# Expert weights of a mixture-of-experts stage loaded as contraction halves, 16 KB a partition, with stationary operands read at a step of four

## The reference, cut to what matters

```python
def expert_block(args):
    xb, e = args
    g = xb @ w_gate[e].astype(jnp.float32) + b_gate[e].astype(jnp.float32)
    u = xb @ w_up[e].astype(jnp.float32) + b_up[e].astype(jnp.float32)
    g = jnp.minimum(g, SWIGLU_LIMIT)
    u = jnp.clip(u, -SWIGLU_LIMIT, SWIGLU_LIMIT)
    act = g * jax.nn.sigmoid(SWIGLU_ALPHA * g) * (u + 1.0)
    return act @ w_down[e].astype(jnp.float32) + b_down[e].astype(jnp.float32)
```

## Time and profile before

| | us |
|---|---|
| timed executions | 2716.2, 2707.0, 2698.15 |
| their median | 2707.0 |
| profiled execution, span from first to last instruction | 2703.2 |
| TensorE busy in it | 2299.3 |

### The profile page before, as it was taken

One profiled execution on the slowest core, in us unless ns is written; L12 is line 12 of the kernel. 1 busy time (PEld: TensorE's weight loads), 2 busy tenths in 40 slices (PEclk: granted clock), 3 DMA queues, 4 the chain that ended last, 5 costly groups with the idle time before them and its releaser, 6 DMA issues.

```text
span 2703.2 us, 25686 instructions
## 1 busy us (share of the span) xinstructions
PE 2299.3 (85%) x10610; PEld 1330.2 (49%) x10611; DVE 651.8 (24%) x995; ACT 360.4 (13%) x547; POOL 108.4 (4%) x117
## 2 busy tenths in 40 slices
PE   3987789799879999997899979779997957867998
PEld 1643346334333344332344337458846747846873
DVE  2657623111111111110111111510004464621000
ACT  1121011111011111110111121210001321211000
POOL 2000010000000000000000010020000011300000
PEclk9898889999989999998999989889997978878999
DMA  9761245899579999995899994034343400003430
GB/s 230 260 249 48 75 168 193 330 360 394 207 272 396 395 394 394 394 379 188 328 394 394 394 330 148 32 110 156 140 145 119 151 5 1 1 32 110 156 109 16
DMA packets 246162, 580.79 MB, mean 215 GB/s; under 512 B 7123, under 2 KB 8163, under 8 KB 245952
## 3 DMA queue, kind: packets, MB, share of 16 engines
q1 hardware_dynamic: 240272, 562.39, 56.4%
q0 software_dynamic: 5808, 17.19, 2.8%
HBM read 578.48 MB, written 1.07 MB: 214 GB/s over the span
## 4 chain that ended last, share of the span: by engine, by line
PE 76%; DVE 9%; DMA 6%; ACT 5%; issue 3%; SPq 1%; another core or an unknown queue 0%; POOL 0%; DVEq 0%; ACTq 0%
PE ps L1157 17%; PE ps L1448 11%; PE ps L1174 8%; PE ps L1459 6%; PE ps L582 6%; PE ps L590 5%; PE ps L1138 4%; DMA ring<-in_w_up 4%; PE ps L1159 2%; PE ps L1180 2%; PE ps L506 2%; DMA ring<-in_ada_w 2%; PE ps L1793 1%; PE ps L1799 1%; PE ps L803 1%
## 5 line engine op out<-in xcount | busy, mean ns | idle before, releaser
L1157 PE MATMUL ps<-ring,arena 128*64 128x512 f32 x1632 | 367.0, 603 | 37.7 <-issue 32.4
L1448 PE MATMUL ps<-arena,ring 128*128 128x256 f32 x1408 | 308.4, 383 | 1.5 <-ACT arena L559 1.5
L1448 PEld LDWEIGHTS ps<-arena,ring 128*128 128x128 f32 x1408 | 270.2, 192 | 39.7 <-ACT arena L559 2.3
L1157 PEld LDWEIGHTS ps<-ring,arena 128*64 128x64 f32 x1632 | 114.2, 139 | 285.5 <-issue 274.3
L1174 PE MATMUL ps<-ring,arena 128*64 128x512 f32 x1088 | 244.4, 601 | 6.0 <-ACT arena L1127 1.5
L1102 DVE TENSOR_SCALAR arena<-ps 128x512 f32<-128x512 f32 x34 | 23.5, 692 | 619.1 <-PE ps L1159 619.1
L1174 PEld LDWEIGHTS ps<-ring,arena 128*64 128x64 f32 x1088 | 90.4, 138 | 138.3 <-issue 138.3
L1459 PE MATMUL ps<-ring,arena 128*128 128x512 f32 x352 | 151.4, 592 | 0.0
L582 PE MATMUL ps<-arena,ring 128*128 128x256 f32 x672 | 149.2, 384 | 0.7 <-ACT arena L559 0.7
L1138 PEld LDWEIGHTS ps<-arena 128*128 128x128 f32 x1120 | 129.3, 194 | 28.2 <-issue 28.2
L1157 PE MATMUL ps<-arena 128*64 128x512 f32 x544 | 126.7, 620 | 17.3 <-issue 17.3
(11 more groups left out here) (442 smaller groups left out, 2097.3 us busy)
## 6 DMA issues: line engine op xcount, KB each, us to landing
ring<-in_w_up SPq DMA_DIRECT2D x64, 2048.0 KB, 15.0
ring<-in_w_down SPq DMA_DIRECT2D x64, 2048.0 KB, 13.5
ring<-in_w_gate SPq DMA_DIRECT2D x32, 2048.0 KB, 22.4
arena<-in_w_gate SPq DMA_DIRECT2D x32, 2048.0 KB, 22.1
ring<-in_ffn_w_gate_up SPq DMA_DIRECT2D x22, 2048.0 KB, 7.9
ring<-in_ada_w SPq DMA_DIRECT2D x12, 2048.0 KB, 19.9
ring<-in_ffn_w_down SPq DMA_DIRECT2D x10, 2048.0 KB, 7.7
ring<-in_w_in SPq DMA_DIRECT2D x8, 2048.0 KB, 19.8
```

The costliest lines, as they stand in the source:

```text
L1157: pe.matmul(bank(i)[h * CAP:(h + 1) * CAP, :], xT[:, k, 0:CAP], w[h][:, k, :], start=(k == 0), stop=False)
L1448: m = pe.matmul(bank(b0 + g)[:, c * SEQ:(c + 1) * SEQ], w[:, k, (2 * g + c) * P:(2 * g + c + 1) * P], hT2[:, k, :], start=(k == 0), stop=( ...
```

## The change

All six transfers of an expert become halves of the contraction: half h of a matrix is rows 512h to 512h+511, all 1024 columns. In a half, partition p takes rows 4p to 4p+3, which lie side by side in memory, so that a partition gets one run of 16 KB. The number of transfers, their 2 MB, their slots, their order and the waits stay.

Step k of the contraction now is rows 512(k//4) + 4p + k%4 in partition p. So `pe_gate_up` takes block k%4 of half k//4 and the columns of h from it. The gather takes every fourth feature of a half of `h2` as the stationary operand, and the transposes in `pe_hidden` every fourth column of `act_`; a new function `every4` gives these views, with a step of 16 bytes. `pe_down` is unchanged, since its transposed hidden columns come in the new order. The order of the instructions is the same on every engine.

```diff
--- before.py
+++ after.py
@@ -1075,13 +1075,17 @@
 
 
         W7 = [RING[:, i * SLOT_W:(i + 1) * SLOT_W] for i in E_SLOT]
-        gate_w = [[x.rearrange("p (k n) -> p k n", k=KD) for x in xs] for xs in (W7[0:2], odd_gate)]
-        up_w = [W7[2 + h].rearrange("p (k n) -> p k n", k=KD) for h in range(2)]
+        gate_w = [[x.rearrange("p (k n) -> p k n", k=4) for x in xs] for xs in (W7[0:2], odd_gate)]
+        up_w = [W7[2 + h].rearrange("p (k n) -> p k n", k=4) for h in range(2)]
         down_w = [W7[4 + h].rearrange("p (k n) -> p k n", k=4) for h in range(2)]
 
         def slot_iota(r, n):
             a = names["slots"][0] + r * 2 * CAP
             return CON[:, a:a + n]
+
+        def every4(x, j):
+
+            return x.rearrange("p (q j) -> p j q", j=4)[:, j, :]
 
         def dve_choose(dve, s, e, r, odd):
 
@@ -1135,7 +1139,7 @@
             pe.wait_ge(s.p_ready, n)
             for k in range(KD):
                 for t in range(TT):
-                    m = pe.matmul(bank(2 + k // 4)[:, (k % 4) * P:(k % 4 + 1) * P], h2[:, t, k * P:(k + 1) * P], Psel[:, t, :],
+                    m = pe.matmul(bank(2 + k // 4)[:, (k % 4) * P:(k % 4 + 1) * P], every4(h2[:, t, k // 4 * 512:(k // 4 + 1) * 512], k % 4), Psel[:, t, :],
                                   start=(t == 0), stop=(t == 1))
                 if k % 4 == 3:
                     m.then_inc(s.x_ps, 1)
@@ -1154,7 +1158,7 @@
                 weights(i)
                 for k in range(KD):
                     for h in range(2):
-                        pe.matmul(bank(i)[h * CAP:(h + 1) * CAP, :], xT[:, k, 0:CAP], w[h][:, k, :], start=(k == 0), stop=False)
+                        pe.matmul(bank(i)[h * CAP:(h + 1) * CAP, :], xT[:, k, 0:CAP], w[k // 4][:, k % 4, h * 512:(h + 1) * 512], start=(k == 0), stop=False)
                 for h in range(2):
                     m = pe.matmul(bank(i)[h * CAP:(h + 1) * CAP, :], Ee[odd], b_[:, h * 512:(h + 1) * 512], start=False, stop=True)
                 m.then_inc(done, 1)
@@ -1162,7 +1166,7 @@
         def pe_hidden(pe, s, n):
             pe.wait_ge(s.a_ready, n)
             for j in range(4):
-                m = pe.transpose(bank(2)[:, j * P:(j + 1) * P], act_[:, j * P:(j + 1) * P], ident)
+                m = pe.transpose(bank(2)[:, j * P:(j + 1) * P], every4(act_, j), ident)
             m.then_inc(s.aT_ps, 1)
 
         def pe_down(pe, s, n, weights, pwT):
@@ -1280,12 +1284,10 @@
             i = ("w_gate", "w_up", "w_down").index(name)
             w = A[name][0][e:e + 1] if isinstance(e, int) else A[name][0][bass.ds(e, 1)]
             for h in range(2):
-                if i < 2:
-                    src, dst = w[:, :, h * 512:(h + 1) * 512], (gate_w[odd], up_w)[i][h]
-                else:
-                    src, dst = w[:, h * 512:(h + 1) * 512, :], down_w[h]
+                dst = (gate_w[odd], up_w, down_w)[i][h]
                 there = odd_ready[h] if i == 0 and odd else slot_ready[E_SLOT[2 * i + h]]
-                sp.dma_start(dst, src.rearrange("a (k p) n -> p (a k) n", p=P)).then_inc(there, 16)
+                src = w[:, h * 512:(h + 1) * 512, :].rearrange("a (p k) n -> p (a k n)", p=P)
+                sp.dma_start(dst.rearrange("p k n -> p (k n)"), src).then_inc(there, 16)
 
         def sp_s7(sp):
             for i, name in enumerate(("w_gate", "w_up", "w_down")):
```

## The result

The changed kernel takes 2831.75 us (median of four, 2828.66 to 2835.14), the kernel before 2703.01 (of four). The ratio is 1.0467 with a 95% interval of 1.0437 to 1.0496: slower by 129 us. The forecast of 2702 us was wrong, and rival A (2825.5) came true. In the rows of the changed kernel TensorE's lines of the expert stage stand four lower: the gather's L1138 is L1142, and L1157 is L1161.

A forecast was written before the change was run, and what follows sets the result against it. TensorE and the weight transfers were both nearly full, with transfers falling 1.1 us an expert behind. Span 2703.2 - 5.5 (transfer waits) + 0 (strided loads) = 2697.7, plus 3.8 outside the span, gave 2702 us; range 2690 to 2838.

The forecast's parts named there:

- rival A: Strided loads of the stationary operand run at half speed: gathers cost 123 us more, transposes about 1; 2825.5 us; chance 0.37.
- Step (4): Stationary operands of gathers and transposes read at a step of four: zero cost, not firmly; at most 123 and 15 us.
- The last line of the prediction: Signs of being wrong: a gather longer than 3.8 us, or pieces called issue ahead of L1161 over 60 us.
- The bound "a column takes twice as long": Upper bound for strided stationary loads: +110 ns on 1120 gather loads, 123 us, and at most 15 us for transposes.
- Step (1): Weight transfers in 16 KB runs: 610 ns a run, 430 GB/s, an expert in 29.3 us; gain 5.5 us.
- the five waits: TensorE's waits for the w_up transfer late in the expert stage, 5.2 us in all, expected to vanish.
- Step (2): SyncE issues 128 descriptors instead of 1024 or 512 and is free sooner; worth nothing.
- Step (3): Moving side of gate and up matmuls: same count, shape, order and contiguous columns, only addresses differ; zero.
- Rival B: Code fetches ahead of expert matmuls get slower behind 16 KB packets, by 70 us; 2771 us; chance 0.08.
- Step (5): Psel, the outputs in PSUM, the copies and the biases stay as before; zero.
- Rival C: Code fetches get quicker with fewer descriptors in the rings; half of 49.7 us goes; 2673 us; chance 0.05.
- Rival D: Long runs strike memory less evenly, all transfer rates stay at 387 GB/s; 2720 us; chance 0.04.

The follow-up runs named there:

- The first experiment: The changed kernel with its 16 KB runs kept but gather and transposes reading side by side, against the kernel before: 2695.14 us against 2707.61, ratio 0.9964.

## Why the prediction was wrong

Step (4) failed: "It has that much in reserve, and I take zero, but not firmly." The term for the loads of the gathers was put at zero and measured 134.7 us: a load takes 329 instead of 192 ns, 137 more, and 122 of them stand in the pace of the gather. The reasoning took a reserve of one kind for another. That a transpose's load of 128 columns is faster (144 ns in the mean, 141 in the median of the earlier trace rows, against 192) says something of how often or how fast the engine takes a column whose data lie side by side; it says nothing of what a column costs that shares its line with no other. The changed kernel shows both loads growing together, 141 to 213 ns and 192 to 329. The rest of the step's working was sound and gave the case that came true: no cover for a slower load, all 35 gathers on the path, and an upper bound of 110 ns a load where the pace grew by 122. The last line of the prediction named the sign, a gather longer than 3.8 us; it is 7.57. The bound "a column takes twice as long" was too low by a little; it is 1.93/0.86, 2.2 times. The transposes at 1.2 us were seen rightly in rival A.

The Trainium skill's rule in Advanced Engine Details and Errata, section SBUF Cachelines, that at least two hits on a 16-byte line are needed, is borne out by these runs: two hits (a step of two) cost 0.89 ns a column against 0.86, one hit 1.93. The prediction had read it and let an analogy from rows about something else outweigh it. That was the error of judgement.

Step (1), the transfers, held: 611 ns a packet where 610 was worked out, 432 GB/s where 430 was, the five waits gone. The extrapolation from two sizes of run, cost a run plus cost a byte, carried over to a size four times the larger one. The first experiment gains about 10 us where 5.5 was the sum; its interval, 5 to 15 us, takes in 5.5, and its issue pieces are 2.3 us shorter. Whether the rest is more than the spread of such runs isn't shown.

Step (2), SyncE: held, and it frees nothing. In the kernel before a pair of gate halves is issued in 0.99 us ahead of the stage (at 384.38) and in 14.82 us within it (at 1058.02), the same bytes in the same runs; so the issue grows with the backlog. That descriptors don't fit is the prediction's reading of this, and no run tests it. Step (3), the moving side: held. L1161 has 7.09 us for 32 matmuls. Its mean of 609 ns instead of 603 isn't its own, since the run with the step in the gather and nothing else has 609 as well. Step (5) held.

Rival B (fetches of code slower behind long packets) is refuted: the pieces went from 49.7 to 48.5 us, and no kernel with runs of 16 KB has more. Rival C had the right sign and the wrong size: by the list of waits the six profiles with runs of 16 KB have 46.7 to 48.5 us of such pieces, the six with runs of 2 and 4 KB 49.4 to 50.4, so 1 to 3 us instead of 28. Rival D is refuted by the rates.

The range held the result, 2831.75, because A was priced from a bound and given its place. There was some luck in that: A itself came to 2825.5, and the range reached 2838 only by doubled transposes, which hardly cost anything (1.2 us), while the gathers cost more than their bound.

## What to carry to other kernels

A longer run in a transfer is worth what waits for the transfer; here that was 5.2 us of waits, in a gain of about 10 of 2707 us. Its price was paid in the layout: a float32 matmul operand at a step of 16 bytes, stationary or moving, costs here about twice the time a column (of 32 bytes too, tried for the stationary one), and if the engine is the bound and the operand is read many times, that is the whole bill. In these runs two elements of each 16-byte line in an operand's walk were enough to keep the price down, and where a layout forces a reorder, do it once, on the engine that is idle there, and not on the one that TensorE is about to wait for.

## What the runs showed that I had not expected

- The price of a load does not follow the distance beyond 16 bytes: 192, 196, 261, 329 and 335 ns for a load of 128 float32 columns at steps of one, two, three, four and eight elements.
- Records differ in the price of a line: 0.89 ns a column for a moving operand, 1.02 for the load of a transpose ((213 - 82)/128, with the same 82 ns taken off, which no run shows for a transpose), 1.93 for the load of a matmul. Why the last is twice the others no run here shows.
- VectorE pays as well: 1.16 us for 512 columns read at a step of 16 bytes, where 1024 side by side take 1.28; 1.94 against 1.23 us for 1024 written at a step of 512 bytes.
- A gap of 1.3 to 2.7 us more for TensorE ahead of a stage (1.16 to 2.48 us, 0.74 to 3.40 us) went with a granted clock of 0.79 instead of 0.91 over the 40 us around it, and the stage began 7 us later in place of 4: the router's matmuls behind the gap took 2.7 us longer.
- The first matmuls after a jump still wait 4.7 to 14.2 us for what I read as code (no run tests that reading), whether 2 KB or 16 KB packets are ahead of it. It is the largest idle item left in the stage, and none of these runs moves it by more than 3 us of 50.
